# Statistics of a LayerNorm split between VectorE, ScalarE and GpSimd

## The reference, cut to what matters

```
def layer_norm(x, g, b):
    xf = x.astype(jnp.float32)
    mu = xf.mean(-1, keepdims=True)
    var = jnp.square(xf - mu).mean(-1, keepdims=True)
    return ((xf - mu) * lax.rsqrt(var + LN_EPS) * g + b).astype(x.dtype)

for l in range(DEPTH):
    mix, ... = mixer_prompt(xp, w_in[l], w_o[l], ...)            # projection, attention, convolution
    xp = layer_norm(DEEPNORM_ALPHA * xp + mix, ln1_g[l], ln1_b[l])
    xp = layer_norm(DEEPNORM_ALPHA * xp + hier_moe(xp, *moe_w), ln2_g[l], ln2_b[l])
```

## Time and profile before

| | us |
|---|---|
| median of 3 runs | 2233.22 |
| lowest and highest | 2231.83, 2237.94 |
| span of the profiled execution | 2234.0 |
| TensorE busy in it | 2021.8 |
| VectorE busy | 704.7 |
| ScalarE busy | 382.9 |
| GpSimd busy | 328.5 |

### The profile page before, as it was taken

One profiled execution on the slowest core, in us unless ns is written; L12 is line 12 of the kernel. 1 busy time (PEld: TensorE's weight loads), 2 busy tenths in 40 slices (PEclk: granted clock), 3 DMA queues, 4 the chain that ended last, 5 costly groups with the idle time before them and its releaser, 6 DMA issues.

```text
span 2234.0 us, 35458 instructions
## 1 busy us (share of the span) xinstructions
PE 2021.8 (91%) x12532; PEld 1222.2 (55%) x12532; DVE 704.7 (32%) x1370; ACT 382.9 (17%) x984; POOL 328.5 (15%) x440
## 2 busy tenths in 40 slices
PE   8999999989988998889599999999899899989890
PEld 5666655567544664445366666555765456545450
DVE  4412176661111111111472123666411111111116
ACT  2001123301111111111110011332011111111110
POOL 1200011111212111111331000110111111111114
PEclk9999999999999999989799999999999899999895
DMA  6610013358999999999434110223799999999964
GB/s 226 180 38 29 19 43 113 132 206 318 370 377 379 397 363 386 367 371 338 165 117 112 38 38 11 90 84 123 283 337 371 372 390 374 372 375 367 375 241 158
DMA packets 99957, 527.60 MB, mean 236 GB/s; under 512 B 14554, under 2 KB 23642, under 8 KB 83058
## 3 DMA queue, kind: packets, MB, share of 16 engines
q1 hardware_dynamic: 86738, 491.52, 58.1%
q0 software_dynamic: 13056, 33.84, 6.2%
HBM read 486.21 MB, written 54.60 MB: 242 GB/s over the span
## 4 chain that ended last, share of the span: by engine, by line
PE 64%; DMA 27%; DVE 4%; issue 3%; ACT 1%; POOL 0%; SPq 0%; DVEq 0%; POOLq 0%; ACTq 0%
DMA arena<-in_w_down 25%; PE ps L568 19%; PE ps L708 8%; PE ps L911 7%; PE ps L868 6%; PE ps L549 4%; PE ps L864 4%; PE ps L905 2%; PE ps L855 2%; PE ps L918 2%; PE ps L655 1%; PE ps L752 1%; PE ps L679 1%; PE ps L838 1%; PE ps L667 1%
## 5 line engine op out<-in xcount | busy, mean ns | idle before, releaser
L568 PE MATMUL ps<-arena 128*128 128x344 f32 x1440 | 421.1, 453 | 0.0
L870 PE MATMUL ps<-arena 128*64 128x256 f32 x1792 | 398.8, 381 | 0.0
L868 PE MATMUL ps<-arena 128*64 128x256 f32 x1792 | 398.8, 381 | 0.0
L568 PEld LDWEIGHTS ps<-arena 128*128 128x128 f32 x1440 | 272.0, 190 | 142.9 <-issue 3.6
L868 PEld LDWEIGHTS ps<-arena 128*64 128x64 f32 x1792 | 240.9, 137 | 144.4 <-issue 23.2
L911 PE MATMUL ps<-arena 128*64 128x512 f32 x448 | 239.3, 684 | 82.6 <-DMA arena<-in_w_down 71.7
L870 PEld LDWEIGHTS ps<-arena 128*64 128x64 f32 x1792 | 240.9, 137 | 0.0
L913 PE MATMUL ps<-arena 128*64 128x512 f32 x448 | 239.7, 685 | 0.0
L1831 POOL DMA_INDIRECT ytok<-arena,scol x64 | 94.8, 1482 | 936.6 <-issue 735.2
L1605 DVE SCALAR_TENSOR_TENSOR arena<-ps,gates,arena 64x256 f32<-64x256 f32 (+1 forms) x128 | 61.0, 477 | 448.2 <-ACT arena L1141 448.2
L708 PE MATMUL ps<-arena 128*128 128x512 f32 x448 | 198.0, 599 | 3.3 <-ACT arena L1089 3.3
(11 more groups left out here) (244 smaller groups left out, 2095.8 us busy)
## 6 DMA issues: line engine op xcount, KB each, us to landing
arena<-in_w_gate SPq DMA_DIRECT2D x64, 2048.0 KB
arena<-in_w_up SPq DMA_DIRECT2D x64, 2048.0 KB
arena<-in_w_down SPq DMA_DIRECT2D x64, 2048.0 KB
arena<-in_w_in SPq DMA_DIRECT2D x36, 512.0 KB, 3.3
arena<-out_y_all SPq DMA_DIRECT2D x16, 512.0 KB, 3.6
xs<-arena SPq DMA_DIRECT2D x16, 512.0 KB, 2.7
ytok<-arena SPq DMA_DIRECT2D x16, 512.0 KB, 3.6
arena<-ytok SPq DMA_DIRECT2D x16, 512.0 KB, 6.6
```

The source lines that it names most:

```text
L568: last = mm(ps[:, 3 * half + ch, 0:CH], wring[:, slot, k * P:(k + 1) * P], xT[:, k, ch * CH:(ch + 1) * CH], start=(k == 0), stop=(k == KD ...
L868: mm(ps[HALF:P, 2 + q, 0:256], xgT[:, slot, k, 0:HALF], wg[slot3][:, k, cols], start=(k == 0), stop=(k == KD - 1))
L870: last = mm(ps[0:HALF, 2 + q, 0:256], xgT[:, slot, k, 0:HALF], wu[slot3][:, k, cols], start=(k == 0), stop=(k == KD - 1))
```

## The change

The statistics of tile 0 stay on VectorE. For tiles 1 to 8 ScalarE makes three instructions: a copy of the tile to a place that nobody reads (`passed_over`), which also gives the sum of each row; the negative mean from it; and the squares of tile plus negative mean, which also give their row sums. They stand at the end of ScalarE's layer, ahead of the next layer's evictions. Three sets of `sums` take turns, so the sum of tile t waits until tile t-3 has been normalised. GpSimd makes the reciprocal deviation from the sum of squares. VectorE makes the two passes of each tile, one tile after the other. The sum of tile t+1 is written ahead of the squares of tile t.

```
--- before.py
+++ after.py
-STEPS_LAYER = 350
+STEPS_LAYER = 334
...
+        sums = sb("sums", [P, 3, 3])
...
+        passed_over = at(14448, 2, DM)
...
@@ scalar, at the end of the loop over the layers
+                def added2(t):
+                    r = slice(0, P if t < NB else NS)
+                    act.wait_ge(s[f"l2_in{t}"], BASE + 16 * (l + 2))
+                    act.wait_ge(s["l2_square"], BASE + NB * l + max(t - 2, 0))
+                    act.wait_ge(s["x2_ready"], BASE + NT * (l + 1) + max(t - 2, 0))
+                    act.wait_ge(s["l2_sum"], BASE + NB * l + t - 1)
+                    nc.scalar.activation(passed_over[r, 0], xin[t][r], ACT.Copy, accum_out=sums[r, t % 3, 0:1]
+                                         ).then_inc(s["l2_sum"], 1)
+
+                def mean2(t):
+                    r = slice(0, P if t < NB else NS)
+                    act.wait_ge(s["l2_sum"], BASE + NB * l + t)
+                    act.wait_ge(s["x2_ready"], BASE + NT * (l + 1) + max(t - 2, 0))
+                    nc.scalar.mul(sums[r, t % 3, 1:2], sums[r, t % 3, 0:1], -1.0 / DM).then_inc(s["l2_mean"], 1)
+
+                def squared2(t):
+                    r = slice(0, P if t < NB else NS)
+                    act.wait_ge(s["l2_mean"], BASE + NB * l + t)
+                    act.wait_ge(s["l2_rstd"], BASE + NT * l + max(t - 1, 0))
+                    act.wait_ge(s["l2_square"], BASE + NB * l + t - 1)
+                    nc.scalar.activation(passed_over[r, 1], xin[t][r], ACT.Square, bias=sums[r, t % 3, 1:2],
+                                         accum_out=sums[r, t % 3, 2:3]).then_inc(s["l2_square"], 1)
+
+                added2(1)
+                mean2(1)
+                for t in range(2, NT):
+                    added2(t)
+                    squared2(t - 1)
+                    mean2(t)
+                squared2(NT - 1)
@@ vector
                 def statistics2(t, r, p):
                     dve.wait_ge(s[f"l2_in{t}"], BASE + 16 * (l + 2))
-                    dve.wait_ge(s["l2_stat"], BASE + NT * l + p)
...
                 def normalised2(t, r, p):
-                    dve.wait_ge(s["l2_stat"], BASE + NT * l + p + 1)
-                    step.link(v.scalar_tensor_tensor(xin[t][r], xin[t][r], mv[r, p % 2, 0:1], lnp[r, 2],
-                                                     ALU.subtract, ALU.mult))
+                    if p == 0:
+                        dve.wait_ge(s["l2_stat"], BASE + l + 1)
+                        shift, by = mv[r, 0, 0:1], ALU.subtract
+                    else:
+                        dve.wait_ge(s["l2_square"], BASE + NB * l + p)
+                        shift, by = sums[r, p % 3, 1:2], ALU.add
+                    step.link(v.scalar_tensor_tensor(xin[t][r], xin[t][r], shift, lnp[r, 2], by, ALU.mult))
                     dve.wait_ge(s["l2_rstd"], BASE + NT * l + p + 1)
...
                 statistics2(0, rows_at[0], 0)
-                for p in range(1, NT):
-                    statistics2(p, rows_at[p], p)
-                    normalised2(p - 1, rows_at[p - 1], p - 1)
-                normalised2(NT - 1, rows_at[NT - 1], NT - 1)
+                for p in range(NT):
+                    normalised2(p, rows_at[p], p)
@@ gpsimd
                 def inverse2(p, rows):
                     r = slice(0, rows)
-                    pool.wait_ge(s["l2_stat"], BASE + NT * l + p + 1)
+                    if p == 0:
+                        pool.wait_ge(s["l2_stat"], BASE + l + 1)
+                    else:
+                        pool.wait_ge(s["l2_square"], BASE + NB * l + p)
+                    pool.wait_ge(s["x2_ready"], BASE + NT * (l + 1) + max(p - 1, 0))
                     settle(pool, s["pool_passed"])
-                    step.link(g.tensor_scalar(rstd[r, p % 2, 1:2], mv[r, p % 2, 1:2], EPS2, None, ALU.add))
+                    if p == 0:
+                        step.link(g.tensor_scalar(rstd[r, 0, 1:2], mv[r, 0, 1:2], EPS2, None, ALU.add))
+                    else:
+                        step.link(g.tensor_scalar(rstd[r, p % 2, 1:2], sums[r, p % 3, 2:3], 1.0 / DM, EPS2,
+                                                  ALU.mult, ALU.add))
```

More of the change, by code:

```diff
@@ L263, in build @@
         s = {n: sem(n) for n in (
-            "const_in", "init", "copied", "ident_in", "xt_mm", "xt_a", "x2_ready", "x2_out", "l2_stat", "l2_rstd",
+            "const_in", "init", "copied", "ident_in", "xt_mm", "xt_a", "x2_ready", "x2_out", "l2_stat", "l2_rstd", "l2_sum", "l2_mean", "l2_square",
             *(f"l2_in{t}" for t in range(NT)), "w_in0", "w_in1", "w_in2", "proj_mm", "act_ev", "rot_used",
@@ L293, in build @@
             "scalar": (
-                "act_ev", "silu_q", "y_q", "ht_a", "ot_ev", "ot_half", "ov_silu", "ov_xa", "p_ready", "pt_ev", "rk_exp", "silu",
+                "l2_sum", "l2_mean", "l2_square", "act_ev", "silu_q", "y_q", "ht_a", "ot_ev", "ot_half", "ov_silu", "ov_xa", "p_ready", "pt_ev", "rk_exp", "silu",
                 "smp_n", "x1t_a", "xg_a", "xt_a", "y_a"),
```

## The result

The changed kernel took 2242.01 us (median of 13 runs) beside 2235.14 of the kernel before on the same chips. The ratio is 1.0027, with a 95% interval of 1.0019 to 1.0035: 6.0 us more, 4.2 to 7.8. It is slower, beyond doubt, but by 0.27%, which lies just under the 0.3% that I had set as the bound of "no change". The forecast was +11.15 us and 2244.3 us: the time lies in the likeliest case's own range (2241.5 to 2247.5), and the size of the change is about half of what I had worked out. That the time lies in the narrower range is partly luck: these runs of the kernel before stand 1.9 us above the 2233.22 from which I had started, and 2233.22 + 6.0 = 2239.2 would have missed it, though not the full range (2236.5 to 2250.5). One of the 13 runs of the kernel before was slow, at 5269.43 us, and doesn't count in the ratio.

The account below looks back on a forecast made before the run. Bounds: ScalarE's third eviction between the layers, VectorE's last pass at the end. 16.02 us lost less 4.87 gained gave +11.15 on 2234.0, or 2245.1; from the runs' median 2244.3, range 2236.5 to 2250.5.

Parts of the forecast that it names:

- the likeliest case: The forecast itself for the whole kernel: +11.15 us, 2244.3 us, own range 2241.5 to 2247.5, chance 0.60.
- The two places: Between the layers, 16.02 us lost behind ScalarE's third eviction; at the kernel's end, 4.87 us gained at VectorE's last pass.
- part 4: Between the layers: the next layer's evictions queue behind ScalarE's new work, first projection at 1125.12 instead of 1109.10, 16.02 us lost.
- Rival D: Between the layers: ScalarE's loop turn and table load cost nothing once warm; -3.3 us, 2241.0, chance 0.04.
- C: Before each layer's first squares: squares need another table, two more loads, +2.6 to +5.2 us, 2247 to 2249.5, chance 0.05.
- part 3: ScalarE's new statistics: 2.45 us a tile, some 2.6 with gaps, hidden behind VectorE and GpSimd below 3.28.
- The period P: Second normalisation: time per tile, 3.28 us, because GpSimd's two instructions each wait for a pass already started; bounds 2.55 and 3.71.
- 13P - 31.5: Total change in us as a function of the period: tile 8's end holds 8P, ScalarE's end 5P.
- rival B: Second normalisation: GpSimd's reads slip between passes, or both instructions lie under the tile before; P = 2.57, +1.9 us, chance 0.16.
- the signs: Timeline marks: VectorE pausing 0.7 us within each tile, GpSimd at 1.0 and 1.5, last layer done after 31 to 32 us.
- Rival A: Second normalisation: GpSimd's first instruction falls under its own tile's pass; P = 3.71, +16.7 us, 2249.9, chance 0.12.
- slower by more than 0.3%: Whole kernel: slower by more than 6.7 us, chance 0.80, against 0.17 for within that bound and 0.03 for faster.

Follow-up runs that it names:

- e1_hoist: The changed kernel with ScalarE's evictions of the next layer's tiles 0 to 2 put between the statistics; 2226.50 us, ratio 0.9954 to the kernel before.
- e3_before_hoist: Control: the kernel before with the same three evictions moved to the end of ScalarE's loop; 2236.46 us, ratio 1.0001.
- e4_free: The changed kernel with nine places for sums and reciprocal deviations, so ScalarE and GpSimd don't wait for normalised tiles; 2232.56 us, ratio 0.9983.
- e7_free_hoist: The changed kernel with the edits of e1_hoist and e4_free together; 2220.29 us, ratio 0.9928 to the kernel before.
- e5_psum: The changed kernel with VectorE's first pass reading its gain from PSUM, so one SBUF input; output isn't the normalisation; ratio 1.4717.
- e12_after_64: The changed kernel with 36 unused bytes ahead of the large working area, putting it on a multiple of 64; 2241.81 us, ratio 1.0021.
- e9_after_pad: The changed kernel with 144 unused bytes a partition ahead of the working area, putting it where e4_free has it; 2239.76 us, ratio 1.0010.
- e13_free_64: e4_free with its working area moved by unused bytes to a multiple of 64 (byte 48256); 2238.58 us, ratio 1.0010 to the kernel before.
- e8_two: e7_free_hoist with tile 1's statistics on VectorE too and the evictions later; 2220.58 us, ratio 0.9927 to the kernel before.

## Why the prediction was right or wrong

**The two places and their bounds: right.** The change lies in them, with opposite signs, as the earlier trace rows had been read; the 50.9 us behind the first projection stayed (50.54), and nothing downstream swallowed the loss (+0.06 in the next 1033 us, though that stretch moves by several us among kernels).

**The queue behind ScalarE (part 4): right, and shown.** `e1_hoist` takes 15.5 us back by order alone, `e3_before_hoist` shows that the order is worth nothing where ScalarE isn't late. The terms, predicted and measured: tile 5's end to ScalarE's last squares 3.83 and 3.68; turn of the loop 2.0 and 1.65; table load 1.30 and 1.29; eviction, turning, eviction 4.13 and 4.20. On the prediction's clock (0.75 us later) the first projection came at 1123.45 instead of 1125.12. That the 1.65 us are the turn of the loop is my reading: the profile has no row there, and no run splits them. Rival D, that turn and load are free once warm, is ruled out by their rows. So is C: no load stands ahead of the first squares. ScalarE's new work (part 3) was put at 1.13 us for the sum, 1.13 for the squares and 2.45 to 2.6 a tile; measured are 1.06, 1.13 and, where nothing holds it up, 2.36 (`e4_free`).

**The period P: right in mechanism, wrong in size.** This is the term that was mis-sized. I had 1.24 + 0.43 + 0.31 + 1.28 + 0.03 (which adds up to 3.29 and stands as 3.28). Measured is 1.28 for the first pass, 0.40 for GpSimd's overhang, 0.11 until VectorE starts, 1.28, and -0.08, since the next pass starts 0.08 before this one's end: 2.99. Two terms carry the error. The 0.31 came from the earlier trace rows, another place, where the second pass also waits for TensorE and for a transfer; here the hand-over from GpSimd takes 0.10 or 0.11, on every tile that waits. Which of those waits makes the 0.31 wasn't tried. And the +0.03 between passes was taken from the gap inside a tile, where the second pass must wait for the first, and not from that behind L1716. The pass of the earlier trace rows ends at 1101.95, and the next row of that timeline, of the kernel before, already had the answer:

```profile
1101.87 1.28 DVE L1706 BATCH_NORM_STATS2 stat<-arena 128x6 f32<-128x512 f32 x2
```

The statistics of the next tile start 0.08 before that end, as the next tile's pass does now: neighbours on VectorE that don't need each other's result overlap by 0.08 us in these rows. In the prediction's own formula, 13P - 31.5, the measured P gives +7.4 us; the two places gave +7.2. The 0.29 that I had too much in P weighs 13 x 0.29 = 3.8 us of the 3.9 between 11.15 and 7.23; the other terms, each off by at most 0.5, nearly cancel. The point from which rival B decides was given as P = 2.94, and 2.99 is just above it; of the margin of 0.34 us 0.05 was left. Three of the signs missed with it: in the last layer VectorE was done after 29.4 us, not 31 to 32, its pause is 0.51 us, not 0.7, and GpSimd's first instruction takes 0.46, not 1.0, since it starts only when ScalarE's squares are done, 0.41 before the end of the pass that holds it up.

**Rival B.** In the kernel after it came true for the last tile only. Ahead of tile 8's squares there is no further sum that waits for a finished tile, so they are done early, and GpSimd's first instruction gets into the pause:

```profile
1116.55 0.18 POOL L1951 TENSOR_SCALAR rstd<-sums 8x1 f32<-8x1 f32 x1
1116.57 1.28 DVE L1754 SCALAR_TENSOR_TENSOR arena<-arena,rstd,lnp 128x1024 f32<-128x1024 f32 x1 [0.51 <-POOL rstd L1953]
...
1119.08 1.27 DVE L1754 SCALAR_TENSOR_TENSOR arena<-arena,rstd,lnp 8x1024 f32<-8x1024 f32 x1
```

Tile 8 takes 2.51 us, without a pause. For the other tiles the reason given against the rival held: the wait for tile t-3 keeps ScalarE from getting ahead, and in `e4_free`, without that wait, the rival's second half came true. Its first half, GpSimd's reads slipping in between passes, came true in such pauses and never as a quick read between back-to-back passes (`e4_free` 1102.15, `e7_free_hoist` 1108.90). The rule of the Trainium skill (SBUF — State Buffer, "Who interferes with whom") is borne out by `e5_psum` in its first half: 0.19 and 0.55 us beside one SBUF input, 0.46 and 1.37 beside two. For the second half, that a GpSimd instruction which is first holds up VectorE, the cases in the pauses (1102.15 against L1754 at 1102.17, 1116.55 against 1116.57) show no delay of VectorE: its pass starts 0.10 after GpSimd's second instruction and takes 1.28, as elsewhere, though some 0.17 us of GpSimd's instruction were still to run.

**Rival A** holds for single tiles: tile 1 of the kernel after has its first GpSimd instruction under its own pass and takes 3.37 us (8.58 - 5.21). I had only seen it as a case for all tiles.

**A term that I had not seen: the landing of tiles 1 and 2.** Before, VectorE takes tile 1 at 1.75 us after the first statistics in every kernel with the old order, and a landing up to then is hidden. ScalarE takes it as soon as it lands, and waits for it: 1.47 after the statistics in the kernel after, 2.28 in `e1_hoist`, 2.58 in `e12_after_64`, 3.88 in `e4_free`. Tile 1 is finished at 8.58, 9.39, 9.68 and 10.98 us accordingly. The two waits in the timeline of `e1_hoist`:

```profile
1094.05 1.29 DVE L1746 BATCH_NORM_STATS2 stat<-arena 128x6 f32<-128x512 f32 x2 [9.57 <-DMA arena<-ytok]
...
1096.33 1.06 ACT L1214 ACTIVATE arena<-arena 128x1024 f32<-128x1024 f32 x1 [11.98 <-DMA arena<-ytok]
```

Tile 2's landing counts too, since its sum stands ahead of tile 1's squares: in `e9_after_pad` tile 1 was there at 1.43, but ScalarE stood 1.02 us for tile 2, and tile 1 was finished at 9.61. With late landings the change costs up to 1.6 us more (`e12_after_64`: 8.8 against 7.2 in the two places), and `e4_free` and `e13_free_64`, the same code but for 20 unused bytes, differ by 2.7 there. Why a tile lands later in one kernel than in another wasn't tried.

**Size and bound.** +7.2 in the two places and -1.2 elsewhere give the +6.0 of the ratio. The case that I had given 0.80, "slower by more than 0.3%", didn't come: the sign was right, but 6.0 us lie 0.7 under the bound of 6.7, in the case that had 0.17. Of the 5.1 us between 11.15 and 6.0 the period carries 3.8; the 1.2 elsewhere are none of my terms. I had also taken 0.3% as what a measurement tells from no change. The interval is narrower (0.16% wide), but what tells an edit from its side effects is wider, by the table above.

## What to carry to other kernels

Work moved to an idle engine isn't free because the engine is idle: ask what it does next in program order, and whether those next instructions (here three evictions, a loop's turn, a table load) had been hidden by the idleness; if so, write them between the new ones. A shared pipeline's period should be summed from the gaps of this place, between the same kinds of neighbours, since an error of 0.3 us a tile was multiplied by 13. Compare stages and not only totals when a change is smaller than what eight unused bytes do.

## What the runs showed of the hardware that I had not expected

- GpSimd's power of a 128x1 column: 0.55 to 0.58 us where VectorE stands still or reads one input from SBUF, 1.34 to 1.49 where it reads two. It ends 0.40 after the pass that it fell under even where VectorE begins the next such pass 0.08 before the end of the first (`e4_free`: L1953 at 1104.88 for 1.49, L1754 ending at 1105.97, the next pass from 1105.89).
- A GpSimd instruction that starts 0.02 before a pass takes 0.19 us, not 0.46, and as long as ScalarE stays ahead it sets the phase of the following tiles: 2.99 became 2.52 us a tile in `e4_free`; in `e8_two`, where ScalarE fell back, 2.99 came again.
- ScalarE: a sum of 1024 elements takes 1.06 us, squares with a bias from SBUF 1.13, and the 0.19 us read of the accumulator overlaps the instruction ahead of it by 0.09 or 0.10. Nothing comes between a table load and the next copy but 0.01 us (1117.21 + 1.28 to 1118.50).
- Eight unused bytes ahead of a buffer changed a kernel of 2235 us by 0.43%, outside the stretches that the edit here touches. Kernels with the buffer at the same byte mostly agree there; by what rule the byte matters these runs don't show.
